# Two two-layer transformer blocks on one core: order of VectorE and ScalarE steps around rotations, scans, block probabilities, head norms and last outputs

## The reference, cut to what matters

```python
o_gla  = gla(q, k, v, g, ...)        # gated linear attention, 4 heads of 64
o_rwkv = rwkv7(r, k, v, w, a, g)     # delta rule, 4 heads of 64
o_nsa  = nsa(...)                    # 8 heads: compressed blocks + selected + window
mix = concatenate([o_gla, o_rwkv, o_nsa]) @ w_out
x = layer_norm(alpha * x + mix)
x = layer_norm(alpha * x + (silu(x @ w_gate) * (x @ w_up)) @ w_down)
```

## Time and profile before

| | us |
|---|---|
| median of 3 runs | 1549.4 |
| lowest, highest | 1549.4, 1552.5 |
| the profiled execution, its own time | 1543.15 |
| its span | 1541.6 |

### The profile page before, as it was taken

How to read it: one execution, slowest core, us unless ns; L and a number is a source line. 1 busy time by engine, 2 the same in 40 slices (tenths; PEclk the granted TensorE clock), 3 DMA queues, 4 the chain that set the end, 5 groups by cost and what they waited for, 6 DMA issues and landing times. The chain is left out here.

```text
span 1541.6 us, 20723 instructions
## 1 busy us (share of the span) xinstructions
PE 1495.2 (97%) x7896; PEld 1232.6 (80%) x7896; DVE 701.9 (46%) x1092; ACT 779.3 (51%) x1232; POOL 961.6 (62%) x416
## 2 busy tenths in 40 slices
PE   7999999999999999999999999999999999899997
PEld 6888788878887888788788768888788797688886
DVE  3222865472137762645665851110347667612112
ACT  5544665445445665358444444443477344454342
POOL 6887538888885468877200278878774002488785
PEclk9999999999999999999999999999999999999999
DMA  7666326555664346565311157655553311366563
GB/s 237 170 184 178 110 84 177 173 173 164 195 178 123 110 124 221 178 189 151 118 56 56 55 151 221 188 156 193 168 161 111 110 56 55 109 178 182 147 199 128
DMA packets 121633, 227.97 MB, mean 148 GB/s; under 512 B 10304, under 2 KB 26176, under 8 KB 121536
## 3 DMA queue, kind: packets, MB, share of 16 engines
q1 hardware_dynamic: 120384, 222.46, 48.3%
q10 hardware_dynamic: 1152, 4.19, 0.9%
HBM read 225.58 MB, written 1.05 MB: 147 GB/s over the span
## 5 line engine op out<-in xcount | busy, mean ns | idle before, releaser
L179 POOL TENSOR_TENSOR parts<-raw,parts 128x1024 fp32r<-128x1024 f32 (+5 forms) x412 | 961.4, 2346 | 565.5 <-ACT parts L172 563.3
L210 PE MATMUL ps<-parts,xT 128*128 128x512 f32 (+4 forms) x2624 | 810.2, 386 | 9.6 <-ACT H L715 3.0
L172 ACT CAST parts<-raw 128x1024 fp32r<-128x1024 f32 (+5 forms) x412 | 416.0, 1012 | 430.1 <-PE ps L210 252.7
L210 PEld LDWEIGHTS ps<-parts,xT 128*128 128x128 f32 x2624 | 487.2, 188 | 114.1 <-issue 5.2
L210 PE MATMUL ps<-parts,x_low 128*128 128x512 f32 (+3 forms) x672 | 251.2, 382 | 0.0
L210 PE MATMUL ps<-parts,M_low 128*128 128x512 f32 (+2 forms) x640 | 244.3, 386 | 0.0
L210 PEld LDWEIGHTS ps<-parts,x_low 128*128 128x128 f32 x672 | 126.7, 189 | 22.9 <-issue 0.5
L210 PEld LDWEIGHTS ps<-parts,M_low 128*128 128x128 f32 x640 | 120.4, 188 | 20.3
L210 PE MATMUL ps<-parts,aT 128*128 128x512 f32 x352 | 109.8, 395 | 0.6 <-POOL parts L179 0.6
L210 PE MATMUL ps<-parts,H_low 128*128 128x512 f32 x272 | 106.0, 394 | 0.0
L210 PEld LDWEIGHTS ps<-parts,aT 128*128 128x128 f32 x352 | 66.0, 187 | 16.7 <-POOL parts L179 1.1
(11 more groups left out here) (351 smaller groups left out, 1802.3 us busy)
## 6 DMA issues: line engine op xcount, KB each, us to landing
raw<-in_w_in SPq DMA_DIRECT2D x160, 512.0 KB, 3.6
raw<-in_ffn_w_down SPq DMA_DIRECT2D x44, 512.0 KB, 4.5
raw<-in_ffn_w_gate SPq DMA_DIRECT2D x40, 512.0 KB, 3.7
raw<-in_ffn_w_up SPq DMA_DIRECT2D x40, 512.0 KB, 3.7
raw<-in_w_out SPq DMA_DIRECT2D x32, 512.0 KB, 3.5
raw<-in_w_branch SPq DMA_DIRECT2D x24, 512.0 KB, 3.4
raw<-in_w_mem_kv SPq DMA_DIRECT2D x16, 512.0 KB, 3.5
raw<-in_w_in SPq DMA_DIRECT2D x16, 366.0 KB, 3.2
```

The source lines that it names most:

```text
L172: self.nc.scalar.copy(self.part(i, 0)[:, 0:nk, 0:w], self.raw(i)[:, 0:nk, 0:w]).then_inc(self.hi_ready.sem, 1)
L179: self.nc.gpsimd.tensor_tensor(self.part(i, 1)[:, 0:nk, 0:w], self.raw(i)[:, 0:nk, 0:w], self.part(i, 0)[:, 0:nk, 0:w], ALU.subtract).then ...
L210: ins = pe.matmul(b[:, 0:w], a(k0 + 2 * n + c, t), self.part(i, lo_w)[:, c, 0:w], start=(opens and n == p == 0), stop=(final and p == len( ...
```

## The change

It has five parts. In the first block, after the last item of column group 11, ScalarE empties the first PJ bank ahead of the cast and the second behind it. In the second block, VectorE rotates the queries ahead of the scans, and ScalarE's two exponentials of the GLA decays move behind the gate sigmoid. `block_sums` moves up and also multiplies the exponentials of the block scores by the factor, so that TensorE turns divided and gated probabilities, and `block_output` is one addition. `weighted` goes: ScalarE makes WG = gate x weight and BG = gate x shift (for RWKV (bonus + shift), times the gate on VectorE) ahead of the norms, into the buffers LD and EP, and `mixed` is one product and one addition. `nsa(13)`, which holds the last output of token tile 1, moves ahead of `spread(0)`, and `turn_n` waits accordingly.

```diff
+LAST_NARROW = ("in", 11)
...
+                        closes = W.begin(s) + n == W.end(s) and s[0] in ("in", "mem")
+                        ahead = closes and s == LAST_NARROW
+                        if ahead:
+                            take(s, 0)
                         W.high(act, W.begin(s) + n + SPLIT - 1)
-                        if W.begin(s) + n == W.end(s) and s[0] in ("in", "mem"):
-                            for t in range(NT):
+                        if closes:
+                            for t in range(1 if ahead else 0, NT):
                                 take(s, t)
...
+        WG, BG = LD, EP
...
                 def block_turn_p():
-                    pe.wait_ge(*E("pc_exp").at(1))
+                    pe.wait_ge(*E("mxc").at(2))
...
                 def turn_n(t):
-                    pe.wait_ge(*E("ns").at((1, 1 + len(SUMS2) // 4)[t]))
+                    if t == 0:
+                        BO.taken(pe, ("block", 0))
+                    else:
+                        pe.wait_ge(*E("ns").at(len(SUMS2) // 4))
...
                 casts(("in", 5), 3)
-                act.wait_ge(*E("cum_g").at(1))
-                lane.done(sc.activation(EP[:, 0:2, :], CUM[:, 0:2, :], ACT.Exp, scale=1.0 / 16), E("exps"))
-                lane.done(sc.activation(EE[:, 0:2, :], EE[:, 0:2, :], ACT.Exp, scale=1.0 / 16), E("exps"))
                 casts(("in", 6), 0)
...
                 lane.done(sc.activation(gate[:, :, :], H[:, :, NGT:NGT + 24], ACT.Sigmoid), E("gate"))
+                act.wait_ge(*E("cum_g").at(1))
+                lane.done(sc.activation(EP[:, 0:2, :], CUM[:, 0:2, :], ACT.Exp, scale=1.0 / 16), E("exps"))
+                lane.done(sc.activation(EE[:, 0:2, :], EE[:, 0:2, :], ACT.Exp, scale=1.0 / 16), E("exps"))
...
+                def gains(g, c0):
+
+                    for c in range(2):
+                        w, b = (vec[:, v0 + c0 + c:v0 + c0 + c + 1] for v0 in (V_LNW, V_LNB))
+                        lane.done(sc.activation(WG[:, c0 + c, :], g[:, c, :], ACT.Copy, scale=w))
+                        if c0:
+                            lane.done(sc.activation(BG[:, c0 + c, :], BON[:, c, :], ACT.Identity, bias=b), E("shifts"))
+                        else:
+                            lane.done(sc.activation(BG[:, c, :], g[:, c, :], ACT.Copy, scale=b), E("shifts"))
+
                 first = W.begin(("out_nsa", 0))
-                nsa(7)
+                turned_p(6)
+                gains(GT, 2)
+                exps(7)
                 W.high(act, first)
-                nsa(8)
+                turned_p(7)
+                act.wait_ge(*E("gg_ok").at(1))
+                gains(FT[:, F_GG:F_GG + 2, :], 0)
+                exps(8)
...
-                weighted(0)
                 squares(1)
                 W.high(act, first + SPLIT + 1)
                 deviation(1)
                 W.high(act, first + SPLIT + 2)
-                weighted(1)
...
                     roped(4, t, K_AT, 384, NKC, E("k_roped"))
+                for t in range(NT):
+                    roped(5, t, 0, 512, NQ, E("q_roped"))
                 dve.wait_ge(*E("lnz").at(1))
                 tt(LD[:, 0:2, :], LD[:, 0:2, :], GQt[:, :, :], ALU.subtract)
                 summed(0)
-                for t in range(NT):
-                    roped(5, t, 0, 512, NQ, E("q_roped"))
...
+                    tt(pc, pc, fcc[:, :, :].unsqueeze(3).to_broadcast([P, NT, 8, NB]), ALU.mult, E("mxc"))
...
-                    BO.empty(lane, v.tensor_tensor(tmp.rearrange("p (h d) -> p h d", d=HD), b.rearrange("p (h d) -> p h d", d=HD),
-                                                   fcc[:, t, :].unsqueeze(2).to_broadcast([P, 8, HD]), ALU.mult), ("block", t))
-                    dst = NS[:, t, :].rearrange("p (g c d) -> p c g d", g=2, c=4)
-                    tt(dst, dst, tmp.rearrange("p (c g d) -> p c g d", c=4, g=2), ALU.add, None if t else E("ns"))
+                    ins = v.tensor_tensor(dst, dst, b.rearrange("p (c g d) -> p c g d", c=4, g=2), ALU.add)
+                    BO.empty(lane, ins, ("block", t))
...
-                    dve.wait_ge(*E("weighted").at(t + 1))
-                    tt(b[:, 0:2], b[:, 0:2], FT[:, F_GG:F_GG + 2, n], ALU.mult)
-                    tt(b[:, 2:4], b[:, 2:4], BON[:, :, n], ALU.add, settle=False)
-                    tt(b[:, 2:4], b[:, 2:4], GT[:, :, n], ALU.mult)
+                    tt(b, b, WG[:, :, n], ALU.mult)
+                    tt(b, b, BG[:, :, n], ALU.add)
...
                 soft(6)
+                block_sums()
                 gla_scale(4)
...
-                tt(FT[:, F_GG:F_GG + 2, :], FT[:, F_GG:F_GG + 2, :], TM, ALU.mult)
-                block_sums()
+                tt(FT[:, F_GG:F_GG + 2, :], FT[:, F_GG:F_GG + 2, :], TM, ALU.mult, E("gg_ok"))
...
                 nsa(9)
+                dve.wait_ge(*E("shifts").at(4))
+                tt(BG[:, 2:4, :], BG[:, 2:4, :], GT[:, :, :], ALU.mult)
                 block_output(1)
...
                 nsa(12)
+                nsa(13)
                 spread(0)
-                nsa(13)
                 n_low(1)
```

More of the change, by code:

```diff
@@ L2430, in block_sums @@
                         ts(fcc[:, t, :], fcc[:, t, :], chip.rowv[:, t:t + 1], None, ALU.mult, settle=t == 0)
+                    tt(pc, pc, fcc[:, :, :].unsqueeze(3).to_broadcast([P, NT, 8, NB]), ALU.mult, E("mxc"))
                 def block_output(t):
                     b = BO.read(dve, ("block", t))
+                    dst = NS[:, t, :].rearrange("p (g c d) -> p c g d", g=2, c=4)
                     lane.settle()
-                    BO.empty(lane, v.tensor_tensor(tmp.rearrange("p (h d) -> p h d", d=HD), b.rearrange("p (h d) -> p h d", d=HD),
-                                                   fcc[:, t, :].unsqueeze(2).to_broadcast([P, 8, HD]), ALU.mult), ("block", t))
-                    dst = NS[:, t, :].rearrange("p (g c d) -> p c g d", g=2, c=4)
-                    tt(dst, dst, tmp.rearrange("p (c g d) -> p c g d", c=4, g=2), ALU.add, None if t else E("ns"))
+                    ins = v.tensor_tensor(dst, dst, b.rearrange("p (c g d) -> p c g d", c=4, g=2), ALU.add)
+                    BO.empty(lane, ins, ("block", t))
                 def level(n, u):
```

## The result

| | before | changed |
|---|---|---|
| median, first reading (4 runs each) | 1549.4 | 1534.7 |
| ratio, first reading | | 0.9895 [0.9865, 0.9925] |
| ratio, two later readings | | 0.9913 [0.9899, 0.9926], 0.9909 [0.9891, 0.9928] |
| mean of all executions | 1548.2 (75) | 1533.9 (14) |
| mean granted clock of these | 0.9904 | 0.9914 |

Faster, as forecast, but by 14.3 us in the mean where 8.0 were predicted, and 1534.7 lies 0.3 us under the range. The profiled pair shows only 9.3 us. The profiled execution of before was a short one, at clock 0.993; across the 75 executions of that kernel 0.001 of clock goes with 1.4 us. The ratios leave out one execution of the kernel before, of 1573.0 us, that held the lower clock level for 61 us at one stretch.

What follows compares the result with a forecast made beforehand. TensorE, busy 97%, was taken as the bound, so only its waits counted; gains of 2.7 + 0.2 + 2.5 + 0.9 + 1.7 = 8.0 us took the median 1549.4 to 1541.4 us, range 1535 to 1548.

Steps and rivals of the forecast that it cites:

- Edit 1: Last narrow projection group: reading the first PSUM bank before the cast removes a 1.38 us wait per layer; gain 2.7 us.
- Edit 2: Query rotations ahead of GLA scans: old waits go, new ones of 1.7 and 2.4 us come; gain 0.2 us in all.
- Edit 3: Block probabilities divided ahead of their turn: waits for softmax exponentials after both block outputs go; gain 2.5 us.
- Edit 5: Norm weights and shifts multiplied into the gates: both 0.88 us waits ahead of the output projection go; gain 1.7 us.
- Edit 4: Last outputs ahead of the variance: output waits go, a 0.6 us wait for the low half comes; gain 0.9 us.
- The gate product meets GpSimd: Second block output: the query-key-sum and gate product waits out a GpSimd subtraction, 2.9 us back, 1544.3 us; chance 0.2.
- The clock lands elsewhere: Shifted times: one clock fall like that at 835 to 841 vanishes or comes, 1538.8 or 1544.0 us; chance 0.15.
- Waits only change hands: Whole kernel: each saving is handed to the next late partner; gain only 2.5 us, 1546.9 us; chance 0.12.
- Slower: Query turns: new waits of 1.7 and 2.4 us bring a lasting clock fall behind them, 1561 us; chance 0.04.

Runs made afterwards that it cites:

- the doubled scans: Changed kernel with the two GLA scans issued twice over; ratio to the kernel before 0.9930 [0.9915, 0.9946].
- edit 5 alone: Kernel before with only the norm weights and shifts multiplied into the gates; ratio 1.0058 [1.0045, 1.0071].
- the version without edit 3: Changed kernel with only the early division of the block probabilities undone; ratio to the kernel before 1.0001 [0.9992, 1.0010].

## Why the prediction was right and where it was wrong

**Edit 1: right.** Both waits gone, the second read costs 0.26 and 0.15 us; 2.8 against 2.7 by the rows.

**Edit 2: the step that failed.** Direction of the argument right, term wrong: "VectorE spends 741.69 - 737.23 = 4.46 us on the subtraction, two scans and difference", "But the scans now stand before the next VectorE step, the block copy", and so "New wait: 1.7 us". The order is as said: the first query turn came on time, the rotations began where they were put (735.09; with the 2.9 us by which that instant was already earlier, 738.0), and the doubled scans showed that the bank hangs on them. But 4.46 us was the length of that stage in its old place, under GpSimd's subtraction. In its new place, with GpSimd idle, it took 2.83. The rotations took 4.95 instead of 5.21. Together 1.9 us less, and the block copy ends as TensorE comes: the new wait of 1.7 us is there, at 0.02 to 0.04. In layer 1 the scans had been held up too (2.89), and the new wait of 2.4 us shrank likewise; the two rotation sums, which the prediction had meet GpSimd at a price of about 1.5 us, took 0.98 and 0.85. The term is 4.8 in place of 0.2, and 4.6 of the 5.7 us by which the sum fell short. The prediction saw the same hold-up at layer 1's subtraction ("contention") and took the merged row of the scans as if it were work. Even its upper bound, 2.6, rested on the block copy's old end, 748.24, which the hold-up had set. The fall of the clock that goes with the old wait in 7 of 18 places, 1.2 us in the mean, is on top; the prediction knew only a profile without one.

**Edit 3: right in its own terms,** 2.7 against 2.5, the turn of the probabilities uncontended: the new product ends at 837.62 and TensorE comes at 840.45, 2.8 us of cover where 2 were given. What the prediction did not see is that this edit decides over edit 5.

**Edit 4: right,** 1.0 against 0.9. The low half waits 0.39 us, not 0.6.

**Edit 5: mechanism right in the whole change, size off.** 2.4 against 1.7, beyond its upper bound of 1.8. The waits' rows say 0.88 each, but the start of the instruction behind moved by 1.05, and 0.1 us more came along around it. The same holds at most waits here: 2.18 in the row and 2.39 on the instructions, 0.59 and 0.66, 1.32 and 1.42. The ends of products are modelled, and the row of a wait is up to 0.3 us short of what the wait costs. With 0.7 for edit 5, 0.4 for edit 2 (part of its 4.6) and 0.2 for edit 3 that is 1.3 of the 5.7 us by which the sum fell short.

**The rivals.** *The gate product meets GpSimd* didn't happen, with 0.3 us to spare on one side. The prediction's gap of "about 1.4 us" is worked out from no row: in before the two subtractions follow each other without one, and edit 3 opened one of 1.6 us. So this outcome, though the likelier on record, was in part luck. Priced at 2.9 us, it costs some 11 when it does (9 us slower where 2.4 were to be won): the term left out is the fall behind it. *The clock lands elsewhere* is true of every execution, and in the mean it went for the change, 0.9904 to 0.9914. *Waits only change hands* is true of 0.26 + 0.15 us at edit 1 and 0.3 a layer at edit 4, no more. *Slower* named a real danger at the wrong place: with edit 5 alone the clock halves for 13.6 us after a new wait of 1.57 us, but behind the second block output, not at the query turns. The page TensorE: Matmul & The Clock Gate of the Trainium skill states, in its section "A second HAM failure mode: psum-queue depth-cycling", that frequent tiny idles between groups of products make the clock swing between its two levels; the prediction named the section before that one, which is about longer waits for data. The runs here show single waits, not frequent ones, and neither bear that out nor refute it: a fall came with waits of 1.57 us, and none with the 1.32 us of the doubled scans.

**The range** failed by 0.3 us: its low end allowed 2.4 us for edit 2, where 4.6 were due, and took nothing for waits that cost more than their rows. Of the 14.3 us in the mean, 13.7 come from the rows and an estimated 1.2 from the falls near the query turns. That is 14.9 together, 0.6 too much, within the spread of the executions.

## What to carry to other kernels

Before you move a step, read its line's least, median and greatest duration, not only the merged row where it stands, and then look up in the timeline where the long ones are: what exceeds the median can be a lock or a wait that belongs to the place and stays behind. A short distance between two engines that is the same in every execution is a hand-over, not room to spare; delay the first and see. And before you put a VectorE step with two SBUF operands into a dense stretch, look at what GpSimd does at that instant; if the answer hangs on tenths of a microsecond, price the case where they meet with the fall of the clock behind it. An edit measured alone may show a loss that another edit of the same change removes, so measure pairs where one moves the instant at which the other runs.

## What the hardware showed that I had not expected

A stretch of 13.6 us at the lower clock level comes with a single wait of 1.57 us ahead of the 64-row score products, in four places of four: both layers of edit 5 alone and both of the version without edit 3. It begins about 0.3 us behind the end of the wait in three of them and 0.25 us before it in the fourth. The waits of 2.18 us at the query turns, longer, brought only 3.4 us, and that in 7 of 18 places; the waits of 1.32 us at the same turns none in two. A longer wait didn't mean a longer fall; what stood behind it differed. Which property of those instructions decides was not tried.
